# The entry to the experts in another order: scores by tokens, ranks behind shared w1, shared down behind pass 0's turning

## The reference

```python
def moe_ffn(u, w_router, b_router, w1, w3, w2, ws1, ws3, ws2):
    scores = jax.nn.sigmoid((xf @ w_router).astype(jnp.float32))      # 256 x 64
    biased = scores + b_router
    # groups of 8: the 4 groups whose two best add up highest; in them the 8 best experts
    _, idx = lax.top_k(jnp.where(expert_mask, biased, NEG_INF), TOP_K)
    w = jnp.take_along_axis(scores, idx, axis=-1)
    w = w / (jnp.sum(w, axis=-1, keepdims=True) + 1e-20) * ROUTED_SCALE
    ...
    out = swiglu(xpad[toks], w1[e], w3[e], w2[e])                      # for each expert, its tokens
    ...
    shared = swiglu(xf, ws1, ws3, ws2)                                 # all tokens
    return (routed + shared)

def swiglu(x, w1, w3, w2):
    return (jax.nn.silu(x @ w1) * (x @ w3)) @ w2
```

## Time and profile before

| | |
|---|---|
| three runs | 2399.28 us median, 2398.68 to 2400.83 |
| the profiled execution | 2398.06 us |
| its span, first to last instruction | 2396.8 us |
| PE busy | 2309.0 us, 96% of the span |
| DVE, ACT, POOL busy | 34%, 24%, 6% |
| DMA | 673.21 MB, mean 281 GB/s |
| experts of layer 0 | from about 371 us to about 920 us |
| experts of layer 1 | from about 1252 us to about 1800 us |

### The profile page before, as it was taken

One profiled execution on the slowest core, in us unless ns is written; L12 is line 12 of the kernel. 1 busy time (PEld: TensorE's weight loads), 2 busy tenths in 40 slices (PEclk: granted clock), 3 DMA queues, 4 the chain that ended last, 5 costly groups with the idle time before them and its releaser, 6 DMA issues.

```text
span 2396.8 us, 34579 instructions
## 1 busy us (share of the span) xinstructions
PE 2309.0 (96%) x14027; PEld 1650.0 (69%) x14027; DVE 814.2 (34%) x2133; ACT 570.1 (24%) x1231; POOL 135.6 (6%) x179
## 2 busy tenths in 40 slices
PE   7999999999998998999999999998989999999998
PEld 4868897676665665768887676666657777854764
DVE  0376623212121111486524122211223544421264
ACT  2234412111111112224211111111113343321264
POOL 4040000000000000100000000000000000000110
PEclk9999999999999999999999999999999999999999
DMA  9785684999999996855776999999993543141110
GB/s 336 273 294 190 228 338 188 408 418 417 417 418 418 418 418 256 309 180 191 285 300 242 407 418 420 418 418 417 418 375 121 182 156 110 71 150 53 71 71 18
DMA packets 194619, 673.21 MB, mean 281 GB/s; under 512 B 14000, under 2 KB 50072, under 8 KB 144528
## 3 DMA queue, kind: packets, MB, share of 16 engines
q1 hardware_dynamic: 187776, 656.87, 70.5%
q0 software_dynamic: 6240, 13.99, 1.7%
q10 hardware_dynamic: 432, 0.01, 0.0%
HBM read 661.38 MB, written 9.45 MB: 280 GB/s over the span
## 4 chain that ended last, share of the span: by engine, by line
PE 88%; DMA 7%; DVE 1%; ACT 1%; issue 1%; SPq 1%; DVEq 0%; ACTq 0%
PE ps L282 49%; PE ps L2175 13%; PE ps L2212 7%; DMA ring<-in_w 7%; PE ps L2228 4%; PE ps L1757 3%; PE ps L1207 1%; PE ps L695 1%; PE ps L2924 1%; PE ps L3537 1%; DMA ring<-in_w_in 1%; PE ps L3702 1%; PE ps L3685 1%; PE ps L2198 1%; PE ps L3694 1%
## 5 line engine op out<-in xcount | busy, mean ns | idle before, releaser
L282 PE MATMUL ps<-hT,ring 128*128 128x256 f32 (+2 forms) x2352 | 541.1, 386 | 3.2 <-ACT ar L1577 1.9
L282 PEld LDWEIGHTS ps<-hT,ring 128*128 128x128 f32 (+1 forms) x2352 | 438.5, 189 | 99.7 <-issue 37.1
L2175 PE MATMUL ps<-ring,ar 128*32 128x256 f32 (+2 forms) x2688 | 314.3, 389 | 8.6 <-DMA ar<-in_w 4.7
L2175 PEld LDWEIGHTS ps<-ring,ar 128*32 128x32 f32 (+2 forms) x2688 | 189.1, 126 | 96.8 <-issue 20.4
L2175 PE MATMUL ps<-ar 128*64 128x256 f32 (+2 forms) x1120 | 179.5, 388 | 9.1 <-DMA ring<-in_w 9.1
L2212 PE MATMUL ps<-ring,ar 128*64 128x512 f32 (+2 forms) x728 | 159.7, 612 | 12.6 <-DMA ring<-in_w 7.3
L2495 DVE TENSOR_TENSOR ar<-ar,ps 128x256 f32<-128x256 f32 x50 | 21.1, 422 | 437.0 <-PE ps L2175 437.0
L2519 DVE SCALAR_TENSOR_TENSOR exact_parts<-ps,ar,exact_parts 128x512 fp32r<-128x512 f32 x100 | 75.1, 751 | 215.0 <-ACT exact_parts L2363 209.4
L282 PE MATMUL ps<-ring,ar 128*128 128x512 f32 x320 | 140.3, 595 | 0.0
L2363 ACT ACTIVATE exact_parts<-ps,ar 128x512 fp32r<-128x512 f32 x100 | 68.7, 687 | 291.0 <-PE ps L2212 272.8
L2175 PEld LDWEIGHTS ps<-ar 128*64 128x64 f32 (+2 forms) x1120 | 102.7, 129 | 46.2 <-issue 11.8
(11 more groups left out here) (461 smaller groups left out, 2813.8 us busy)
## 6 DMA issues: line engine op xcount, KB each, us to landing
ring<-in_w SPq DMA_DIRECT2D x259, 1024.0 KB, 21.1
ar<-in_w SPq DMA_DIRECT2D x100, 1024.0 KB, 18.5
ring<-in_w_mod SPq DMA_DIRECT2D x36, 2048.0 KB, 11.9
ring<-in_w_in SPq DMA_DIRECT2D x28, 2048.0 KB, 12.0
ring<-in_ab_w_in SPq DMA_DIRECT2D x46, 1024.0 KB, 11.3
cst<-in_w SPq DMA_DIRECT2D x25, 1024.0 KB, 18.0
ring<-in_w_out SPq DMA_DIRECT2D x4, 2048.0 KB, 10.1
ar<-in_ab_w_in SPq DMA_DIRECT2D x8, 1024.0 KB, 24.5
```

The lines of the kernel that those rows point to most:

```text
L282: ins = te.matmul(o, l, r, start=(first and i == 0), stop=(last and i == len(pairs) - 1), skip_group_check=lax)
L2175: ins = te.matmul(b[cols, 0:256], K.x_b[:, kk, in_pair(p, cols)], w[r][:, kk, :], start=(kk == 0), stop=(kk == 7))
```

## The change

Everything concerns the entry and is done in both layers.

- **Scores by tokens.** The router multiplies with blocks of h as the stationary operand, two products of 128 tokens x 64 experts for each of eight steps, into banks 7 and 6. ACT takes the sigmoid straight from them, in two instructions. Copy and turning of the logits go.
- **Shared w1 and w3 as two items** of one unit, each with its own event of landing and of release. PE does both halves of w1, then later w3 in halves (`pe_shared_w3`). The shared products sit in banks 2 and 3.
- **Ranks** are asked for behind shared w1, ahead of shared w3.
- Between the halves of w3: slots of passes 0 and 1, and the lists turned. After the second half: h turned (banks 6, 0, 1, 5), the lists ranked, the selected tokens.
- **Shared down** (`pe_shared_down`) follows the turning of pass 0, all of it at once.
- DVE does the places first, then selects, ranks and slots, then the shared products and low parts (`dve_rows`), then the ranked lists, then the copies of the selected tokens. ACT copies the turned lists between its two silus.
- `RING_HELD` has new times: w1's unit -4 as before, w3's -2 instead of -4, down's 0.75 instead of -2.

```diff
-NOTHING, THIRD, OUT, ROUTER, SHARED_UP, SHARED_DOWN = -12, -10, -8, -6, -4, -2
+NOTHING, THIRD, OUT, ROUTER, SHARED_W1, SHARED_W3, SHARED_DOWN = -12, -10, -8, -6, -4, -2, 0.75
...
-    rb = yield from K.bank(("logits", l), only=7)
+    rb = []
+    for i in range(2):
+        rb.append((yield from K.bank(("scores", l, i), only=7 - i)))
...
-        ins = te.matmul(rb[0:64, 0:256], w[:, kk, :], h[:, kk, :], start=(kk == 0), stop=(kk == 7))
-    ins.then_inc(*K.pe("logits_ps", l, ps=rb))
+        for i in range(2):
+            ins = te.matmul(rb[i][:, 0:64], h[:, kk, i * P:(i + 1) * P], w[:, kk, :], start=(kk == 0), stop=(kk == 7))
+    ins.then_inc(*K.pe("logits_ps", l))
...
+    w = k_major(K.flat["ws1", l], 256)
+    te.wait_ge(*(yield ("ring", "ws1", l)))
+    for j in range(2):
+        b = K.ps["shared", l, j] = yield from K.bank(("shared_g", l, j), only=2 + j)
+        pairs = [(w[:, kk, j * P:(j + 1) * P], h[:, kk, :]) for kk in range(8)]
+        ins = products(te, b[:, 0:256], pairs)
+    ins.then_inc(*K.pe("used", "ws1", l))
+    te.wait_ge(*(yield ("ring", "ws3", l)))
     b = yield from K.bank(("places", l), ("counted", l), only=7)
     te.wait_ge(*(yield ("chosen", l)))
...
-    w2 = k_major(K.flat["down", l, EXPERTS], D, 2)
+    pe_shared_w3(K, l, 0, range(8))
+    yield from pe_first_slots(K, l)
+    yield from pe_lists_turned(K, l)
+    pe_shared_w3(K, l, 1, range(8))
+    for q in range(2):
+        for i in range(2):
+            b = yield from K.bank(("hx_lo", l, i, q), only=(6, 0, 1, 5)[2 * q + i])
+            for k in range(4):
+                ins = te.transpose(b[:, k * P:(k + 1) * P], h[:, 4 * q + k, i * P:(i + 1) * P], K.ident)
+            ins.then_inc(*K.pe("h_turned", l, i, q, ps=b))
+    yield from pe_lists_ranked(K, l)
+    yield from pe_selected(K, l, 0)
...
-        if n == 1:
-            yield from pe_first_slots(K, l)
-            yield from pe_selected(K, l, 0)
-            yield from pe_lists_turned(K, l)
-    ins.then_inc(*K.pe("shared_down", l))
-    K.pe.also("used", "down", l, EXPERTS)
-    yield from pe_lists_ranked(K, l)
+    ins.then_inc(*K.pe("used", "down", l, EXPERTS))
...
         yield from pe_turn(K, l, p)
+        if p == 0:
+            yield from pe_shared_down(K, l)
...
+def dve_rows(K, l):
+
+    ve = K.ve
+    for j in range(2):
+        ve.wait_ge(*(yield ("shared_silu", l, j)))
+        ve.tensor_tensor(K.gs[:, j, :], K.ss[:, j, :], K.ps["shared_up", l, j][:, 256:512],
+                         ALU.mult).then_inc(*K.dve("shared_g", l, j))
+    ve.wait_ge(*(yield ("h_turned", l, 1, 1)))
+    for q in range(2):
+        for i in range(2):
+            cols = slice(q * 512, (q + 1) * 512)
+            ve.wait_ge(*(yield ("hx_hi", l, i, q)))
+            ve.tensor_tensor(K.hx_lo_r[:, i, cols], K.ps["h_turned", l, i, q][:, :], K.hx_hi[:, i, cols],
+                             ALU.subtract).then_inc(*K.dve("hx_lo", l, i, q))
...
         for p in range(2):
             yield from dve_slots(K, l, p)
+        yield from dve_rows(K, l)
+        yield from dve_ranked(K, l)
         yield from selected(0)
         yield from dve_select(K, l, 2)
-        yield from dve_ranked(K, l)
         yield from dve_select(K, l, 3)
```

More of the change, by code:

```diff
@@ L438, in shared @@
     def shared(l):
-        K.plan(("up", l, EXPERTS), 2, [(lambda f: f[:, 0:UNIT], I["ws1"][l].rearrange("(p k) f -> p (k f)", k=8)),
-                                       (lambda f: f[:, UNIT:2 * UNIT], I["ws3"][l].rearrange("(p k) f -> p (k f)", k=8))])
+        for n in ("ws1", "ws3"):
+            K.plan((n, l), 1, [(lambda f: f, I[n][l].rearrange("(p k) f -> p (k f)", k=8))])
         K.plan(("down", l, EXPERTS), 1, [(lambda f: k_major(f, D, 2), I["ws2"][l].rearrange("(j p) n -> p j n", j=2))])
@@ L1908, in pe_moe_start @@
         te.wait_ge(*(yield ("h", ("ffn", l), kk, 0)))
-        ins = te.matmul(rb[0:64, 0:256], w[:, kk, :], h[:, kk, :], start=(kk == 0), stop=(kk == 7))
-    ins.then_inc(*K.pe("logits_ps", l, ps=rb))
+        for i in range(2):
+            ins = te.matmul(rb[i][:, 0:64], h[:, kk, i * P:(i + 1) * P], w[:, kk, :], start=(kk == 0), stop=(kk == 7))
+    ins.then_inc(*K.pe("logits_ps", l))
     K.pe.also("used", "router", l)
[L1912 to L1925, removed]
-    for i in range(2):
[L1927 to L1931, removed]
+    for i in range(2):
+        K.ps["logits_ps", l, i] = rb[i]
+    w = k_major(K.flat["ws1", l], 256)
[6 more added lines that the diff above has]
+    te.wait_ge(*(yield ("ring", "ws3", l)))
     b = yield from K.bank(("places", l), ("counted", l), only=7)
@@ L1939, in pe_moe_start, with pe_shared_w3, pe_shared_down @@
                                     for i in range(2)]).then_inc(*K.pe("ranks", l, ps=b))
-    w2 = k_major(K.flat["down", l, EXPERTS], D, 2)
+    pe_shared_w3(K, l, 0, range(8))
[10 more added lines that the diff above has]
+    yield from pe_selected(K, l, 0)
+def pe_shared_w3(K, l, j, of):
+    w, b = k_major(K.flat["ws3", l], 256), K.ps["shared", l, j]
+    ins = products(K.te, b[:, 256:512], [(w[:, kk, j * P:(j + 1) * P], K.h[:, kk, :]) for kk in of],
+                   first=(0 in of), last=(7 in of))
+    if 7 in of:
+        ins.then_inc(*K.pe("shared_up", l, j, ps=b))
+    if j == 1:
+        K.pe.also("used", "ws3", l)
+def pe_shared_down(K, l):
+    te, w2 = K.te, k_major(K.flat["down", l, EXPERTS], D, 2)
     te.wait_ge(*(yield ("ring", "down", l, EXPERTS)))
@@ L1997, in act_moe_start @@
     ac.wait_ge(*(yield ("logits_ps", l)))
[L1998 to L2001, removed]
+    for i in range(2):
+        ac.activation(K.sc[:, i, :], K.ps["logits_ps", l, i][:, 0:64], ACT.Sigmoid).then_inc(*K.act("scores", l, i))
     for j in range(2):
@@ L2004, in act_moe_start @@
         ac.activation(K.ss[:, j, :], K.ps["shared_up", l, j][:, 0:256], ACT.Silu).then_inc(*K.act("shared_silu", l, j))
-    for i in range(2):
-        for q in range(2):
+        if j == 0:
+            ac.wait_ge(*(yield ("lists_ps", l)))
+            ac.activation(K.turned_lists[0:64], K.ps["lists_ps", l][0:64, :].rearrange("p (a n) -> p a n", a=4),
+                          ACT.Copy).then_inc(*K.act("lists_turned", l))
+    for q in range(2):
+        for i in range(2):
             ac.wait_ge(*(yield ("h_turned", l, i, q)))
@@ L2020, in dve_moe_start @@
     ve.wait_ge(*own())
-    ve.wait_ge(*(yield ("scores", l)))
+    ve.wait_ge(*(yield ("scores", l, 1)))
     ve.tensor_tensor(bi, sc, K.brow[l].unsqueeze(1).to_broadcast([P, 2, 64]), ALU.add).then_inc(*K.dve())
@@ L2071, in dve_moe_start @@
     ve.tensor_copy(K.tok_w[:, :, :, 1], mk).then_inc(*K.dve())
[L2072 to L2082, removed]
     ve.wait_ge(*(yield ("ranks", l)))
@@ L2341, in act_experts @@
         yield from selected(0)
-        ac.wait_ge(*(yield ("lists_ps", l)))
-        ac.activation(K.turned_lists[0:64], K.ps["lists_ps", l][0:64, :].rearrange("p (a n) -> p a n", a=4),
-                      ACT.Copy).then_inc(*K.act("lists_turned", l))
     for p in of:
```

4 lines of the change are left out of this document (2 added, 2 removed).

## The result

The changed kernel takes **2404.91 us** (median of 22 runs, 2398.81 to 2410.29); the kernel before, in 22 runs beside it, 2398.97 us. The ratio is 1.0027, 95% interval [1.0021, 1.0033]: 6.5 us or 0.27% slower by the ratio, 5.9 us by the medians. I had predicted 2400.0 us and no change that can be told, with 2403.8 us as the upper end. The prediction was wrong.

What follows compares the result with a forecast made beforehand. PE (96% busy) bounds the kernel, with the weight stream beside it in the experts, started by PE's arrival at pass 1. Terms sum to +0.36 us a layer, +0.7 in all: median 2399.28 to 2400.0, range 2396.8 to 2403.8.

Steps and rivals of the forecast that it cites:

- the half clock: Rival, chance 0.21: at the router or turning of h through ranking, half clock holds 3.4 us longer, costing 1.7 us.
- the router's term: Router by tokens takes 5.15 us against 5.32, a gain of 0.2 us a layer, half clock ending at 374.39.
- the logits' turning: After the router, PE no longer turns the logits: 0.26 us gained a layer.
- The second place: Turning of h, wait and ranking, 4.4 us with little matmul: half clock may hold, price 1.7 us; rival's chance 0.21.
- The sum of the order: Start of pass 1, all terms together, per layer: +0.36 us.
- Mask: Ranks behind shared w1: mask at 382.0, PE there at 383.1, so no wait, 1.0 us to spare.
- The third rival: Change does not do what it says: open table load or late mask makes PE wait, 0.4 us, 2400.8; chance 0.05.
- Turning of h and wait before the ranking: Turning gains 0.16 us from free banks; PE then waits 0.93 for bank 6, held until DVE's low part.
- Wait for pass 0's x: Before pass 0's w1: new wait for DVE's copies of the selected tokens, 0.94 us, bounds 0.7 to 1.4.
- Turned product's copy covered: Shared down behind pass 0's turning covers the copy of the turned product: 0.89 us gained.
- Pass 1's start sets the stage: PE's arrival at pass 1, 419.90 us before and about 420.2 predicted, starts the gapless weight stream.
- the dip: Weight queue empties near 438 us, DMA share 0.50 from 438 to 439; predicted to be wider than before.

Runs made afterwards that it cites:

- the same with the wait filled: Kernel before with the router by tokens alone, plus four dense products in PE's 2.23 us wait for the norm at the router: 2397.33 us, 0.9993.
- bank 7: First turned part of h in bank 7 instead of 6: changed kernel 2403.34 us, 1.0025; changed kernel with the router by experts 2398.28 us, 0.9998.
- the filled kernels with the new order and with the old: Four dense products in PE's wait for the norm at the router: changed kernel 2396.76 us, 0.9999; kernel before 2397.66 us, 0.9995.
- all remedies: Changed kernel with four dense products in the norm's wait, h's first turned part in bank 7, shared down halved around pass 0's turning: 2394.08 us, 0.9981.

## Why the prediction was wrong

**The failed step: the chance given to the half clock.** The mechanism stood there as a rival, in both its places, with 2403.4 and 2406.8 us for once and twice a layer; 2404.91 lies between. I gave it 0.21 and let the range end at 2403.8. What spoke against it was that "the router's stretch has always been followed by full clock". That was read from a router with 256 moving columns to a weight load, and carried over to one with 64. The new router alone, 1.0033, and the same with the wait filled, 0.9993, show that this was the property the change removed. I had seen the sparser work, named it, and then weighed the old kernel's history higher. In the sum it is the router's term that fails: -0.20 us a layer, with the half clock taken to end at 374.39 as before. With the router alone the entry takes 51.73 and 51.76 us against 48.97 in both layers before, +2.8; without the logits' turning, -0.26, the router's term was +3.0 in each.

The size was off as well. I let the half clock last for one more stretch, 1.7 us; in six of ten entries it lasts two more, 3.4 us, and into shared w1, whose products have 256 columns as before. Against that it is not there in every entry, which no row of before could show.

**The second place** got its price right (5.54 - 3.90 = 1.6 us) and its chance not. The row I held against it, 3.5 us of turning and rank products at full clock, has no idle time in it; the stretch I compared it with has 0.8 us. Full clock in twelve entries without it and half in three of eight with it point there. It is shown for the old router in the new order alone, where one bank number takes 1.0029 to 0.9998; in the changed kernel the clock fell there in one of six entries, and bank 7 brought no gain that can be told. The Trainium skill ("TensorE: Matmul & The Clock Gate", Part 4) says that transposes don't count as PE being busy in the same way, and by that rule, as the prediction has it, this place drops. No run here shows the rule by itself: with bank 7 the same 16 transposes and the ranking, back to back, kept the full clock. Whether the transposes had a part in the falls behind the idle time stays open.

**The sum of the order**, +0.36 us a layer, came out as 47.97 - (48.98 - 1.7) = +0.7, the kernel before taken at full clock. Point by point, as differences of starts on PE:

- Router: 3.59 us at full clock against 3.56. I had 5.15 against 5.32 with its half clock, but 5.32 is the row's duration; by starts it is 5.26, and my term should have been -0.1; the double I took for small products at half clock holds (16 in a stretch of 3.40 us). Logits' turning: -0.26, as said.
- Mask: DVE makes it by 379.33, PE asks at 380.06, no wait. The table load ran from 372.17 to 373.45, nearly all of it under the router, which ends at 373.1. The third rival is out.
- Turning of h and wait before the ranking: +0.68, I had -0.16 + 0.93 = +0.77. The wait was 0.78.
- Wait for pass 0's x, together with the selection: +1.24, in layer 1 +1.10; I had 0.94. The wait itself is the 0.94 in the row, so the rest is the selection's. The row puts the wait down to issue, not to DVE; DVE's last copy runs from 398.06 to 398.75, and PE goes on at 398.96, so the copy as its end is my reading.
- Turned product's copy covered: -0.78, I had -0.89. Shared down in one piece: -0.20, I had nothing.

DVE's and ACT's rows for the mask, from the timeline:

```profile
372.17 1.28 ACT L2012 ACT_TABLE_LOAD   x1
...
373.91 0.29 DVE L2037 TENSOR_TENSOR ar<-ar,par 128x128 f32<-128x128 f32 x1 [2.11 <-ACT ar L2012]
...
379.04 0.29 DVE L2072 TENSOR_TENSOR ar<-ar 128x128 f32<-128x128 f32 x1
```

**The rest held.** Pass 1's start sets the stage, and the dip is wider. Pass 0's w1 gave its slot earlier and w2's where it did: SP issues at 402.66 what it issued at 411.30 in the earlier trace rows. The order's own cost, twice 0.7, is not shown by times: the filled kernels with the new order and with the old are 0.9999 and 0.9995.

**Open.** Why the four dense products bring the kernel before 1.2 us, where its entries are 3.3 shorter and its mean clock, 0.9911 against 0.9901 beside it, says 2.4; the interval, 3.4 faster to 1.0 slower, holds both. Why the router alone costs 7.9 us against the kernel before, where its entries are 5.6 longer; the interval is 2.9 us either way. Why bank 7 brought the changed kernel no clock. And what decides in a given entry between 10.2 us of half clock and none: each kernel has one profile (the changed one two), and runs of the changed kernel spread over 11.5 us, those with all remedies over 3.7.

## What to carry to other kernels

When a change makes a stretch behind a wait of PE sparser, with fewer moving columns to a weight load, or puts a wait into such a stretch, price the clock first: what the clock did behind idle times of 0.8 and 2.2 us cost here more than all the instructions and waits of the reordering together, some 4 us against an estimated 1.4. Look whether the rows that kept their full clock had the same shape and no idle time in them, or they prove nothing. Where PE waits anyway, a few dense products into a bank that is about to be overwritten can keep the clock up: here in 12 of 12 entries. See that they start as soon as PE is free; in layer 1 they stood 1.06 us and put the router off by 0.6.

## What the runs showed of the chip

- Behind the same idle time of 2.23 us the granted clock stood at 1.2 GHz for 10.2 us in six of ten entries with 64-column products first (6.8 in one, none in three), and for 3.4 us in all six with 256-column products first. PE had no idle time within the 10.2 us, and up to 5.3 us of 256-column products ran at half in them too (layer 1 of the changed kernel, 1254.46 to 1259.8). With the wait filled, the router by tokens kept the full clock in all ten entries, the one by experts in both.
- At half clock a 128 x 128 weight load with 64 moving columns takes 0.21 us, at full 0.11.
- An idle time of 0.78 us between transposes and small products was followed by half clock in three of eight entries; 0.35 us, or none, in none of twelve.
